# Turned K leaves PSUM by ScalarE, K's last turns follow K, the logits' turn follows the first tile of V

## What is computed

```
h  = rms_norm(x) * (1 + scale) + shift
hq, hf, hi, hg, fq, fk, fv, ff = split(h @ w_in)        # eight column groups
hg_out, state = hgrn_mixer(hq, hf, hi, hg)              # gated linear recurrence, 4 heads x 128
logf = log_sigmoid(ff + bias); c = cumsum(logf)         # one value per row and head
s = q k^T / 8 + c_q - c_k, causal;  o = softmax(s) v    # forgetting attention, 8 heads x 64
x = x + gate * (concat(hg_out, rms_norm(o)) @ w_out)
x = x + gate * moe(rms_norm(x) ...)                     # 16 experts, 2 for each row
```

## Time and profile before

| | us |
|---|---|
| median of 3 runs | 761.65 (760.85 to 765.82) |
| the profiled execution | 763.68 |
| its span, first to last instruction | 761.9 |
| TensorE busy in the span | 663.1 (87%) |
| VectorE, ScalarE, GpSimd busy | 378.4, 210.6, 208.6 |
| mean granted TensorE clock | 0.944 of full speed |

### The profile page before, as it was taken

How to read it: one execution, slowest core, us unless ns; L and a number is a source line. 1 busy time by engine, 2 the same in 40 slices (tenths; PEclk the granted TensorE clock), 3 DMA queues, 4 the chain that set the end, 5 groups by cost and what they waited for, 6 DMA issues and landing times. The chain is left out here.

```text
span 761.9 us, 19146 instructions
## 1 busy us (share of the span) xinstructions
PE 663.1 (87%) x7487; PEld 437.6 (57%) x7487; DVE 378.4 (50%) x1055; ACT 210.6 (28%) x425; POOL 208.6 (27%) x336
## 2 busy tenths in 40 slices
PE   2999999998859999998899992699999999999910
PEld 0686467444536577665755552566676666676710
DVE  3200003458867732465644447545555555555556
ACT  4320026531250211366301120132323232323203
POOL 1111120365503010310100000243444444444440
PEclk9999999999987999999799995799999999999975
DMA  8973565503003323650293129699999999999624
GB/s 315 405 298 111 220 249 206 211 14 112 31 28 131 127 61 132 245 179 1 79 424 157 77 100 401 261 414 412 414 416 413 416 411 405 409 413 412 240 71 182
DMA packets 38417, 182.95 MB, mean 240 GB/s; under 512 B 5912, under 2 KB 6312, under 8 KB 22672
## 3 DMA queue, kind: packets, MB, share of 16 engines
q1 hardware_dynamic: 29968, 158.88, 52.7%
q0 software_dynamic: 8384, 23.12, 8.4%
HBM read 169.57 MB, written 15.28 MB: 243 GB/s over the span
## 5 line engine op out<-in xcount | busy, mean ns | idle before, releaser
L1780 PE MATMUL bank<-weights,x_hT 128*128 128x512 f32 x256 | 111.3, 593 | 0.0
L1764 PE MATMUL bank<-x_hT,weights 128*128 128x272 f32 x384 | 89.5, 394 | 0.0
L2075 PE MATMUL bank<-weights,R 128*32 128x256 f32 x1408 | 80.6, 379 | 4.8 <-issue 3.7
L1780 PEld LDWEIGHTS bank<-weights,x_hT 128*128 128x128 f32 x256 | 48.1, 190 | 59.6 <-issue 59.6
L1764 PEld LDWEIGHTS bank<-x_hT,weights 128*128 128x128 f32 x384 | 72.3, 190 | 16.8 <-issue 1.9
L854 POOL DMA_INDIRECT y_d<-R,x_hT x44 | 51.1, 1160 | 96.1 <-DVE R L1592 45.7
L2075 PEld LDWEIGHTS bank<-weights,R 128*32 128x32 f32 x1408 | 53.9, 110 | 28.4 <-issue 6.8
L1099 ACT ACT_TABLE_LOAD x44 | 56.5, 1283 | 21.0 <-DVEq L1202 20.3
L1099 ACT ACTIVATE R<-bank 128x128 f32<-128x128 f32 x44 | 12.3, 279 | 175.3 <-PE bank L2075 175.3
L848 POOL DMA_INDIRECT R<-h_d,x_hT x46 | 48.1, 1046 | 45.5 <-POOL x_hT L867 28.8
L2004 PE MATMUL bank<-weights,x_hT 128*128 128x512 f32 x128 | 58.6, 610 | 0.0
(11 more groups left out here) (345 smaller groups left out, 955.5 us busy)
## 6 DMA issues: line engine op xcount, KB each, us to landing
weights<-in_w_ada SPq DMA_DIRECT2D x24, 1024.0 KB, 11.1
weights<-in_w_exp_gate SPq DMA_DIRECT2D x16, 1024.0 KB, 11.0
weights<-in_w_exp_down SPq DMA_DIRECT2D x16, 1024.0 KB, 11.2
weights<-in_w_exp_up SPq DMA_DIRECT2D x16, 1024.0 KB, 11.0
R<-in_w_exp_down SPq DMA_DIRECT2D x16, 1024.0 KB, 10.9
weights<-in_w_in SPq DMA_DIRECT2D x7, 2048.0 KB, 9.0
R<-in_w_exp_up SPq DMA_DIRECT2D x8, 1024.0 KB, 11.1
R<-in_w_exp_gate SPq DMA_DIRECT2D x8, 1024.0 KB, 11.0
```

What stands on the lines that cost most here:

```text
L1764: ins = T.matmul(bank[b][:, 0:HALF], w[:, k, h * P:(h + 1) * P], hT[:, k, c * HALF:(c + 1) * HALF], start=(n == 0), stop=(n == KT - 1))
L1780: ins = T.matmul(bank[b][:, :], hT[:, k, i * P:(i + 1) * P], w[:, k, :], start=(k == 0), stop=(k == KT - 1))
L2075: ins = T.matmul(bank[2][32 * j:32 * j + 32, 0:2 * P].rearrange("p (w f) -> p w f", w=2), XT[:, k, :], W2[:, :, k, j * P:(j + 1) * P], sta ...
```

## The change

In the schedule the turn of the logits, `lfT`, moves from behind the last tile of K to behind the first tile of V. With this the turns `fkT` 3 and 4 come directly behind the last tile of K. All five `fkT` are emptied by ScalarE instead of VectorE, at the same places of the schedule.

```diff
         schedule = [("hgrn", -1), ("fk", 0), ("fk", 1), ("fkT", 0), ("hgrn", 0), ("fk", 2), ("fkT", 1), ("ff",), ("fk", 3), ("fkT", 2),
-                    ("fk", 4), ("lfT",), ("fkT", 3), ("fkT", 4), ("hgrn", 1), ("fv", 0), ("fv", 1), ("hgrn", 2),
+                    ("fk", 4), ("fkT", 3), ("fkT", 4), ("hgrn", 1), ("fv", 0), ("lfT",), ("fv", 1), ("hgrn", 2),
             elif item[0] == "fkT":
-                grp(f"fkT{item[1]}", 3, "dve")
+                grp(f"fkT{item[1]}", 3, "act")
             for item in schedule:                # ScalarE's program
                 if item[0] == "fk":
                     evict_k(item[1])
+                if item[0] == "fkT":
+                    i = item[1]
+                    n = ROWS[i]
+                    filled(act, f"fkT{i}")
+                    read("act", f"fkT{i}", A.copy(fkT[:, :, i * P:i * P + n], bank[3][:, :].rearrange("p (a b) -> p a b", a=4)[:, :, 0:n]))
             for item in schedule:                # VectorE's program
-                if item[0] == "fkT":
-                    i = item[1]
-                    n = ROWS[i]
-                    filled(dve, f"fkT{i}")
-                    read("dve", f"fkT{i}", V.tensor_copy(fkT[:, :, i * P:i * P + n], bank[3][:, :].rearrange("p (a b) -> p a b", a=4)[:, :, 0:n]))
                 if item[0] == "ff":
                     fox_sums()
```

## The result

Before ran at 763.07 us and the changed kernel at 759.47, medians of 19 runs each. The ratio estimated from all these runs is 0.9949 (95% interval 0.9933 to 0.9966; the two medians alone give 0.9953), 3.9 us less (2.6 to 5.1). A second comparison gave 0.997 (0.995 to 0.999), 2.3 us less. The profiled execution took 757.83 with a span of 756.1; TensorE is busy for 661.6 of it (88%).

The account below looks back on a forecast made before the run. TensorE, busy for 87% of the span, was taken as the bound, with a 9.92 us stretch holding about 2 us of work. Gain 5.2 − 0.4 = 4.8 us from the median 761.65 gives 756.8, range 753.7 to 759.8.

Parts of the forecast that it names:

- The stall: TensorE between K's last tile and tile 2's small products: these start 5.2 us earlier (5.0 to 5.6).
- The Trainium skill's rule against ScalarE: `fkT` copies: at three times VectorE's 0.68 us, about 2.9 us more, some 759.7; not counted in the sum.
- The logits' turn: Its five transposes, now between two dense V products, cost 0.4 us (bounds 0 and 0.62).
- Queues: Behind the stall: GpSimd held until about 246, sums loaded near 254.5, cost 0; rival of GpSimd's queue as bound, 0.03.
- ScalarE's slack ahead of `kT1`: ScalarE's idle ahead of emptying `kT1` shrinks from 7.74 us to about 0.7, at cost 0.
- the sign of being wrong: Small products start on time but the first expert load, expected about 5 us earlier, doesn't move.
- The clock: After about 3.5 us without TensorE work it falls again; small products stay at 0.50, 5.25 us; worth 0.
- a clock that doesn't fall: Rival: TensorE stays at 2.4 GHz through tile 2's small products, 2.3 us more gain, 754.5; chance 0.08.
- The unexplained idle stretches: Rival: small products, ten instructions fewer ahead, meet an idle stretch set by program place; up to 2.2 us return, 759.0; 0.11.
- The one per cent: Whole kernel: 7.6 us as about what a measurement can tell from no change; under 754.0 counts as faster.

Follow-up runs that it names:

- second comparison: The unmodified change timed again against the kernel before, beside two kernels with tiny added products: ratio 0.997 (0.995 to 0.999).
- two single edits: Against the kernel before: ScalarE emptying `fkT` in the old order, 0.9986; the new order with VectorE still emptying `fkT`, 0.9993.
- second pair of traces: The kernel before and the change each traced once more, nothing edited: second to third set of small products 38.74 and 33.56 us.
- the four wide products: Changed kernel with four 512-column products ahead of the turn of K's fourth tile and four early filler products removed: 0.9921 against the kernel before.
- the changed kernel filled: Changed kernel with 14 extra 128x128 identity products in the empty stretch ahead of the turn of K's fourth tile: 0.9983 against the kernel before.
- the shifted kernels: The change, and its version with softplus behind, each with 25 tiny 32x32 products at the start and 38 in the gap: 0.9912 and 0.9896.
- the kernel before filled: Kernel before with 25 extra 128x128 identity products in the 6.25 us ahead of the logits' turn: 1.0051 against the kernel before.
- the one with the logits late: Changed kernel with the logits' turn put off further, behind V's last tile: 0.9925 against the kernel before.
- the kernel with the softplus behind: Changed kernel with ScalarE's Abs, Exp, Ln behind its copy of `fkT4` and `kT1`'s copy ahead of the exponentials: 0.9895 against the kernel before.

## Why the prediction was right

**The stall.** The gain to the small products is 5.19, against 5.2 (5.0 to 5.6; the starts listed in the working give only 5.0 to 5.2, so the upper bound had no step behind it). ScalarE's queue came as listed: K's copy, `fkT1` straight behind it at 0.59 (0.609 taken), Ln at 221.07 (220.52 forecast; half a microsecond of this lies ahead of the change), K's fourth tile, `fkT2`'s copy. The two single edits show that the mechanism is the one described: bank 3's order and VectorE's queue.

**The Trainium skill's rule against ScalarE.** The prediction's estimate from "ScalarE: Activation LUTs", section "Rules for kernel authors", in the Trainium skill was that the copies cost about 2.9 us more. They didn't. ScalarE's copy in place takes 0.57 to 0.59 us against VectorE's 0.67 to 0.68; the rule's figure is for bf16 and doesn't give the price of this float32 form.

**The logits' turn.** Two V tiles with the turn between them take 247.70 − 233.31 = 14.39 us, without it 252.79 − 238.96 = 13.83. It costs 0.56, near the upper bound of 0.62; I took 0.4.

**Queues.** GpSimd was held to 246.71 (about 246) and loaded the sums at 251.54 (about 254.5), at no cost. ScalarE's slack ahead of `kT1` shrank to 0.47 (0.7 forecast) and held. The first expert load came 6.73 us earlier, so the sign of being wrong that the prediction named, a load that doesn't move, is absent.

**The clock.** It fell again, and the small products took 5.20 (5.25). One thing it put at nothing: the fall begins at about the same time (223.2 before, 223.4 after) but is about 6.8 us long instead of 13.6, so the turn and outputs behind it took 0.92 less. In the second pair of traces the falls are as long, but that of before began earlier, and only 0.18 of this shows. From the second to the fourth set the first pair has 61.89 and 56.34, the second 61.31 and 56.51. The gain in the stage is 5.55 and 4.80. The rival priced a clock that doesn't fall at 2.3 us; the four wide products show about 1.2. "TensorE: Matmul & The Clock Gate", section "HAM oscillation", in the Trainium skill says that gaps in TensorE's work send it back to half rate. The fall behind the gap of 3.50 us agrees; in the changed kernel filled the clock fell with no gap above 0.95, which the rule doesn't cover.

**The unexplained idle stretches.** The rival's premise, that such a stretch depends on the place in the program, holds (the shifted kernels), but the change didn't meet it: ten instructions fewer ahead of the third set left the list of waits at 4.1 us.

**The size.** I forecast 4.8 us; the runs show 3.9 (2.6 to 5.1) and 2.3 (0.8 to 3.8). The two traced pairs give 5.8 and 5.0 (spans 761.9 to 756.1 and 760.8 to 755.8), but the traced executions of the change lie below its median. Part of that is the clock: over 69 runs of the kernel before, the time spent at half clock (the span times one minus the mean clock, twice) explains most of the scatter, 0.37 us of span for 1 us (correlation 0.91). It is 82.4 us on average over 31 runs of the change, but 75.6 and 78.6 in its two traced ones. The mean span of those 31 runs is 757.33, that of the 69 is 760.81, a step of 3.5. Between this and the 4.6 that 5.19 − 0.56 give, about 1 us is open.

The clock is the likely place, though no run shows it. The average time at half clock fell from 85.0 to 82.4, by 2.6 us, where the fall in the stage alone became 6.8 shorter in the traces; so the runs of the change spend some 4 us more at half clock elsewhere. At 0.22 us of span for each (the slope within the 31 runs) to 0.37 this would cost 0.9 to 1.6 us, an estimate. The fall at 175.6 is one such place: both traces of the change have it (16.07 us to the second set, both times) and both of before lack it (15.02 and 15.03). But nothing shows that the change brings it, since the kernel before filled has it and the one with the logits late doesn't.

So the mechanism came as forecast, and the size fell short by 1.3 us of 4.8 over all runs. That the first comparison, 0.9949 of 761.65 or 757.8, lies within 1 us of the forecast 756.8 is partly luck: the second gave only 2.3 us, about half of the forecast step. The one per cent that the prediction took as the least that can be told from no change was too wide: the interval 0.9933 to 0.9966 doesn't contain 1.

## What to carry to other kernels

Where a shared buffer is emptied by an engine with a long serial job in its queue, look at both the engine and the order: here each edit alone was worth 1 to 2 us in its stage and nothing that the runs' times could show, and both were worth 5. The wait that is left names the next edit: behind the copies stood ScalarE's softplus, and moving it gave another 3.7 us in the stage. Extra products that are meant to hold the clock should not change the number of instructions ahead of dense small work, or be few and wide: fourteen small ones left the kernel at 0.9983, four wide ones at 0.9921.

## What the hardware showed that was not expected

TensorE stands idle for 0.2 to 2.3 us at some of the places that lie about 254 instructions apart, or a multiple of it, where they fall into dense small products; 100 added instructions that do nothing moved these stretches from the first two sets of small products into the last two.

The clock can fall to 0.50 while TensorE shows no idle time at all. Stretches of the kernel with the softplus behind, in the turn, outputs and state of the sample tile and the Q block behind them, which no edit here touches:

```profile
289.50:294.50 5.00, 5.00 (x32) 2.88 (x31) 0.24 (x2) 2.07 (x10) 0.00 (x0) 1.00 0.01 2
294.50:297.50 3.00, 3.00 (x8) 2.18 (x8) 2.62 (x15) 0.00 (x0) 0.00 (x0) 0.50 0.00 0
```

All 5.00 us ahead of the fall are busy, with 32 matmuls in them. In the kernels before and after the same work runs at 1.00, in both traces of each; both single edits, the kernel before filled and the one with the logits late show the fall there too. So it comes in some traces and not in others, and a filled gap is no promise of a held clock.
